# First mixer's projection with 512-column matmuls and folds on VectorE, and its first head's gate work one piece later

## The chip, the cores and the metric

One core of a Trainium2 chip runs the whole program. The metric is device time in microseconds (us), the median of several executions. The kernel before takes 2714.08 us (three executions, 2713.33 to 2714.75).

## The reference

Two decoder layers on 256 tokens with model width 2048, in float32. Layer 0 mixes tokens with a gated linear recurrence (8 heads of 256 channels), layer 1 with a state-space mixer; each is followed by a SwiGLU block and a gated per-layer embedding. What the change touches is the mixer of layer 0:

```python
xy = u @ w_in                                  # 2048 x 4096: this is phase A1
xr, yg = jnp.split(xy, 2, axis=-1)
yg = jax.nn.gelu(yg, approximate=True)
xr = causal_dwconv(xr, conv_w, conv_b)         # 4 taps
r = sigmoid(xb @ w_gate_r + b_gate_r)          # 256 x 256 for each head
i = sigmoid(xb @ w_gate_i + b_gate_i)
log_a = -8 * r * softplus(-lam); a = exp(log_a)
bterm = sqrt(-expm1(2 * log_a)) * (i * xr)
h[t] = a[t] * h[t-1] + bterm[t]                # scan over the tokens
y = h * yg                                     # then y @ w_out: phase A2
```

Here xb is xr by heads, and the `u` that enters is an RMS-normalised x.

## The kernel before

**Precision.** Each float32 operand is split in two parts, hi (rounded to the matmul's type) and lo (the rest), and a product is hi·hi + hi·lo + lo·hi. ScalarE makes the hi part of a weight piece (`hi`, L634), VectorE the lo part (`lo`, L915). TensorE does the three products of a 128x128 block in one of two forms. In the narrow form (`three`, L402 to L404) they are three matmuls of 256 columns into the same 256 columns of a bank. In the wide form (phases in the tuple `WIDE`, L419 and L421) one matmul of 512 columns multiplies the hi weights with the hi and lo tokens side by side into a bank's two halves, and one of 256 columns adds lo weights times hi tokens to the first half; whoever reads the bank must add the halves. `fold` (L1104) does this with one TENSOR_REDUCE on VectorE. The result is scaled by `rinv`, the norm of the token (a row is a tensor of 128 channels x 256 tokens).

**Order.** The program is a list of phases. A1 is the first: 4 iterations of 16 pieces, a piece being 8 blocks of weights (512 KB); an iteration holds two heads, and a head's 8 pieces make four groups of 16 blocks, two for xr (groups 0 and 1) and two for yg (2 and 3), each in its own bank. A2 follows with 32 pieces. Weights pass through a ring of 4 slots: SyncE's queue (SP) starts the load of a piece when the lo part four pieces back is made, ScalarE makes hi when TensorE has finished the piece four back, and VectorE lo. The loops of ScalarE and VectorE run over the same pieces as TensorE's, and at step q they split the piece q+3 (`LEAD`). Nothing plans the order: each engine executes its own written list, in order, and waits on semaphores.

**What a head needs beside its projection.** At the steps of its own 8 pieces (s = q % 8) VectorE reads group 0, 1, 2, 3 at s = 1, 3, 5, 7 (L1206 for xr into `xpad`, L1218 for yg into `yv`), does the convolution's later taps at s = 2 and 4 (`later_taps`, L1114 and L1116; the first tap is ScalarE's, L791), splits its input for the gates (`x_low`, L1005, at s = 4 and 6; `gates_low`, L1011, the gate weights, at s = 5). After the last piece of the head TensorE does the 24 gate matmuls, when both `x_low` of the head are done:

```python
pe.wait_ge(g_lo, head + 1)
pe.wait_ge(xc_lo, head * 2 + 2)
```

The rest is a chain one head later, `chain_step(head - 1, ...)`, shared between ScalarE and VectorE: ScalarE at s = 0 the gates' tanh (L702), at 1 the decays and a square (L711 to L721), at 3 the gelu's tanh (L729), at 5 a square root (L725), at 7 the hi part of y (L733); VectorE at s = 2 (L1124), 4 (L1129, L1133), 5 (L1137), and at 6 the input, the scan and y (L1141 to L1146). At the next s = 0 ScalarE starts with the hi part of a weight piece and then the next head's gates' tanh.

**First iteration.** Engines start with x and the norm still to come. The pieces of the first head come in another order (`HEAD_ORDER`), and its groups are read at q = 4 to 7. Its 24 gate matmuls stand after piece q = 9, its tanh is at q = 9 and its decays at q = 10, gelu at 11. On VectorE, `kk_steps(7)` (L933 to L1039, 13 small operations that make the decay's constants) stands at the end of q = 7, and `x_low` of the first head at q = 7 and 8.

Of the kernel before, what the change touches and what calls it, by code (L numbers as in the profile page):

```python
# [26 lines left out]
ALU = mybir.AluOpType  # L27
# [3 lines left out]
SEQ = 256  # L31
# [20 lines left out]
LAST_HEAD = {0: (0, 1), 1: (2, 3), 2: (4,), 3: (5,), 4: (6,), 5: (7,)}  # L52


WIDE = ("A2", "F1", "F2", "B2")
LAST = ((0, 4), (4, 4), (8, 4), (12, 2), (14, 2))
GELU_C = 0.7978845608028654
GELU_S = 0.044715 ** 0.5
# [65 lines left out]
def trunk(nc, t, out):  # L124
    with ExitStack() as ctx:
# [274 lines left out]
        def _(pe):  # L400
# [73 lines left out]
            for index, ph in enumerate(phases):  # L474
# [43 lines left out]
                def body(it, first, ph=ph, name=name, norm=norm, operand_ready=operand_ready):  # L518
# [5 lines left out]
                    for q, w in enumerate(ph["widths"]):  # L524
# [11 lines left out]
                        if name == "B1" and ph["half"] == 0 and first:  # L536
                            if q == 1:
                                decay_products()
                            if q == 9:
                                decay_columns()  # L540
                        if name == "A1" and q in ((9, 15) if first else (7, 15)):

                            head = it * 2 + q // 15 if first else it * 2 + q // 8
                            pe.wait_ge(g_lo, head + 1)
                            pe.wait_ge(xc_lo, head * 2 + 2)
                            if not (first and q == 9):
                                pe.wait_ge(gate_t, head * 4)
                            b = 0
                            for g in range(2):
                                for m in range(2):  # L550
                                    for k in range(2):
                                        tile, c = 16 + b // 2, slice((b % 2) * 128, (b % 2) * 128 + 128)
                                        mm = three(bank[4 + g][:, m * SEQ:(m + 1) * SEQ], R[1][:, 0, tile, c],
                                                   R[1][:, 1, tile, c], R[1][:, 0, 20 + k, :], R[1][:, 1, 20 + k, :],
                                                   k == 0, k == 1)
                                        b += 1
                            mm.then_inc(g_used, 1)
# [64 lines left out]
        def _(act):  # L622
# [38 lines left out]
            for index, ph in enumerate(phases):  # L661
# [73 lines left out]
                def chain_step(head, hh, s):  # L735

                    if s == 0:
                        gates(head)
                    elif s == 1:
                        decays(head)  # L740
                        gelu_square(head, hh)
                    elif s == 3:
                        gelu(head, hh)
                    elif s == 5:
                        mult(head)
                    elif s == 7:
                        lru_y(head, hh)

                def body(it, first, ph=ph, name=name, n=n, index=index):
                    last = isinstance(it, int) and it == ph["iters"] - 1  # L750
                    for q in range(n):
# [9 lines left out]
                            split_dt_weights(q // 13)  # L761
                        if name == "F2" and ph["half"] == 1 and last and q == 1:
                            split_p_high()
                        if name == "A1" and first and q == 9:
                            act.wait_ge(kk_done, 2)
                        if name in PAIRED and next_norm(ph) is not None and q > 8:
                            j = q - 9
# [17 lines left out]
                        if name == "A1":  # L785
                            head, hh, s = it * 2 + q // 8, q // 8, q % 8
                            taps_at = {5: 0, 6: 1} if first and q < 8 else {2: 0, 4: 1}
                            if s in taps_at:
                                j = taps_at[s]
                                act.wait_ge(bank_free, it * 8 + ph["group0"] + 4 + hh * 4 + j + 1)  # L790
                                nc.scalar.activation(xc[:, hh, j, :], xpad[:, j, 3:3 + SEQ], ACT.Identity,  # L791
                                                     bias=flat(apar[:, at(head * 2 + j), 4:5]),
                                                     scale=flat(apar[:, at(head * 2 + j), 3:4])).then_inc(atap_done, 1)
                            if not (first and q < 8):
                                chain_step(head - 1, 1 - hh, {0: 8, 1: 0, 2: 1}.get(s, s) if first else s)
                            if s in ((6, 7) if first and q < 8 else (3, 5)):
                                j = s - 6 if first and q < 8 else s // 5
                                act.wait_ge(xc_done, head * 2 + j + 1)
                                if not (first and q < 8):
                                    act.wait_ge(g_used, head)  # L800
                                nc.scalar.activation(R[1][:, 0, 20 + j, :], xc[:, hh, j, :], ACT.Copy).then_inc(xc_hi, 1)
                            if s == (2 if first and q < 8 else 4):
                                act.wait_ge(g_landed, head * 16 + 16)
                                if not (first and q < 8):
                                    act.wait_ge(g_used, head)
                                nc.scalar.activation(R[1][:, 0, 16:20, :],
                                                     graw[:, 0:1024].rearrange("p (k t) -> p k t", k=4), ACT.Copy
                                                     ).then_inc(g_hi, 1)
# [98 lines left out]
        def _(dve):  # L907
            own = Chain(dve, dve_own)
            V = nc.vector
# [119 lines left out]
            def kk_steps(q):  # L1029

                if q == 1:
                    softplus_mid(1, kt_b, kk_w, kk_z, kk_r)
                elif q == 7:
                    softplus_tail(kt_c, kk_w, kk_z, kk_r)
                    V.tensor_scalar(lam, kt_c, -4.0, None, ALU.mult).then_inc(kk_done, 1)
                    V.tensor_scalar(apar[:, :, 5:7], apar[:, :, 5:7], 0.5, None, ALU.mult).then_inc(kk_done, 1)

                    dve.wait_ge(params_in, 32)
                    own.link(V.tensor_scalar(bpar[:, :, 0:30], bpar[:, :, 0:30], 0.5, None, ALU.mult))  # L1039

            for index, ph in enumerate(phases):
# [60 lines left out]
                def fold(number, dst):  # L1102

                    own.link(V.tensor_reduce(dst, bank[number][:].rearrange("p (s t) -> p t s", s=2), mybir.AxisListType.X, ALU.add))  # L1104
# [44 lines left out]
                def body(it, first, ph=ph, name=name, n=n, index=index):  # L1149
                    last = isinstance(it, int) and it == ph["iters"] - 1  # L1150
                    for q in range(n):
# [31 lines left out]
                        if name == "A1":  # L1183
                            head, hh, s = it * 2 + q // 8, q // 8, q % 8
                            if s == 0 and not first:
                                y_low(head - 2, hh)
                            if first and q in (7, 8):
                                x_low(0, 0, q - 7)
                            if not (first and q < 8):
                                if s == 4:  # L1190
                                    x_low(head, hh, 0)
                                if s == 5:
                                    gates_low(head)
                                if s == 6:
                                    x_low(head, hh, 1)
                                chain_step(head - 1, 1 - hh, {2: 8, 3: 2}.get(s, s) if first else s)

                            group = ({4: 0, 5: 1, 6: 2, 7: 3} if first and q < 8 else {1: 0, 3: 1, 5: 2, 7: 3}).get(s)
                            if group is not None:
                                dve.wait_ge(w_used, HEAD_DONE[group] if first and q < 8 else p - s + 2 * group + 2)  # L1200
                                src = BANKS4[group]
                            if group in (0, 1):
                                j = group
                                tile = head * 2 + j
                                row = xpad[:, j, 3:3 + SEQ]
                                V.tensor_tensor(row, bank[src][:, 0:SEQ], rinv[:], ALU.mult).then_inc(bank_free, 1)  # L1206
                            taps_at = {5: 0, 6: 1} if first and q < 8 else {2: 0, 4: 1}
                            if s in taps_at:
                                j = taps_at[s]
                                tile = head * 2 + j  # L1210
                                dve.wait_ge(atap_done, tile + 1)
                                later_taps(xpad[:, j], xc[:, hh, j, :],
                                           lambda k, tile=tile: flat(apar[:, at(tile), k:k + 1]), xc_done)
                            if group in (2, 3):
                                if group == 2 and not first:
                                    dve.wait_ge(y_lo, head * 2 - 2)
                                row = yv[:, hh, group - 2, :]
                                V.tensor_tensor(row, bank[src][:, 0:SEQ], rinv[:], ALU.mult).then_inc(bank_free, 1)  # L1218
                            if first and q == 7:
                                kk_steps(q)  # L1220
                        if name in ("A2", "F2", "B2"):
                            per = n // 4
                            if q % per == per - 1 if name == "F2" else q >= 8:
# [146 lines left out]
                        V.scalar_tensor_tensor(out=zt[:, j, :], in0=zt[:, j, :], scalar=flat(bpar[:, at(group), 34 + j:35 + j]),  # L1370
                                               in1=grms[:], op0=ALU.mult, op1=ALU.mult).then_inc(yn_done, 1)

                steps(dve, ph, body, own, {"A1": 14, "B1": 22, "F1": 6, "PL": 0, "F2": 4}.get(name, 8))
                own.close()
            dve.wait_ge(h_done, 2 * KT)
            V.tensor_tensor(swi_u[:, 0, :], h[:, KT - 1, :], h[:, KT - 1, :], ALU.mult).then_inc(last_square, 1)
# [181 lines left out]
```

## Time and profile before

| what | value |
|---|---|
| median of three executions | 2714.08 us |
| the profiled execution | 2714.77 us |
| its span, first to last instruction | 2712.6 us |
| outside the span | 2.17 us |
| TensorE busy | 2680.7 us (99%) |
| VectorE busy | 1986.1 us (73%) |
| ScalarE busy | 1362.3 us (50%) |
| DMA, mean | 186 GB/s |
| granted TensorE clock, mean | 0.996 |

The page's busy times are averages over stages. Phase A1 lies in the first 235 us of the span, A2 behind it. Matmuls are pipelined: a record of a matmul is 0.28 us long, but they start 0.12 us apart, so distances between starts say how fast TensorE works, and records' lengths don't.

### The profile page before, as it was taken

The page shows a single profiled execution, that of the slowest core. Times are in us where ns is not written, and L with a number is a line of the kernel's source. Part 1 is how long each engine was busy: PE and PEld are TensorE (multiplying, and loading weights), DVE is VectorE, ACT ScalarE, POOL GpSimd, SP SyncE. Part 2 cuts the span into 40 slices and gives each one's busy share as a digit, 9 for nine tenths or more (in the row PEclk, how much of TensorE's full clock was granted, in tenths as well). Part 3 has the DMA queues.
Part 4 walks back from the last instruction along what each step waited for, and adds up shares of the span by engine and source line. Part 5 has one row for each costly group of instructions (what it writes and reads, how often), then busy time and mean ns, then how long its engine had stood idle before and what let it go on. Part 6 is the DMA issues. An engine that isn't in the chain of part 4 may idle for free.

```text
span 2712.6 us, 49802 instructions
## 1 busy us (share of the span) xinstructions
PE 2680.7 (99%) x17831; PEld 2454.5 (90%) x17831; DVE 1986.1 (73%) x2758; ACT 1362.3 (50%) x1832; POOL 306.9 (11%) x344
## 2 busy tenths in 40 slices
PE   8999999999999999999999999999999999999998
PEld 8999888888888889999998999988888888888897
DVE  6787776665666678888886788877666556666775
ACT  6776444444444444456664566644444444444453
POOL 1001300000000111200001000032000000001222
PEclk9999999999999999999999999999999999999999
DMA  5545565556665566555555655555555665555664
GB/s 198 186 163 194 177 196 188 190 175 188 206 190 188 191 188 194 186 173 190 183 187 180 205 179 183 186 179 187 190 190 181 182 206 189 188 190 175 189 196 136
DMA packets 154241, 504.70 MB, mean 186 GB/s; under 512 B 17104, under 2 KB 21520, under 8 KB 152976
## 3 DMA queue, kind: packets, MB, share of 16 engines
q1 hardware_dynamic: 154048, 503.14, 57.7%
q8 instruction: 70, 1.15, 0.2%
q14 instruction: 43, 0.35, 0.0%
q10 hardware_dynamic: 80, 0.07, 0.0%
HBM read 500.97 MB, written 2.16 MB: 185 GB/s over the span
## 4 chain that ended last, share of the span: by engine, by line
PE 95%; DVE 2%; ACT 1%; DMA 1%; issue 0%; SPq 0%; POOL 0%; DVEq 0%; POOLq 0%; ACTq 0%
PE bank L419 42%; PE bank L421 21%; PE bank L402 10%; PE bank L403 10%; PE bank L404 10%; DVE wlo L915 1%; ACT whi L634 0%; PE bank L597 0%; DMA wraw<-in_A 0%; DMA wraw<-in_B 0%; PE bank L588 0%; PE bank L599 0%; PE bank L575 0%; PE bank L580 0%; DVE arena L1114 0%
## 5 line engine op out<-in xcount | busy, mean ns | idle before, releaser
L419 PE MATMUL bank<-R,whi 128*128 128x512 f32 x4992 | 1734.1, 393 | 0.0
L915 DVE TENSOR_TENSOR wlo<-wraw,whi 128x1024 fp32r<-128x1024 f32 (+2 forms) x1008 | 1179.3, 1176 | 587.1 <-ACT whi L634 585.3
L634 ACT ACTIVATE whi<-wraw 128x1024 fp32r<-128x1024 f32 (+2 forms) x1008 | 985.6, 983 | 974.6 <-PE bank L421 738.3
L421 PE MATMUL bank<-R,wlo 128*128 128x256 f32 x4992 | 1390.4, 279 | 0.0
L419 PEld LDWEIGHTS bank<-R,whi 128*128 128x128 f32 x4992 | 935.1, 187 | 213.1 <-issue 0.3
L421 PEld LDWEIGHTS bank<-R,wlo 128*128 128x128 f32 x4992 | 940.2, 188 | 0.1
L402 PE MATMUL bank<-R,whi 128*128 128x256 f32 x2368 | 678.3, 286 | 6.8 <-DVE wlo L915 4.7
L403 PE MATMUL bank<-R,whi 128*128 128x256 f32 x2368 | 670.0, 283 | 0.0
L404 PE MATMUL bank<-R,wlo 128*128 128x256 f32 x2368 | 669.9, 283 | 0.0
L402 PEld LDWEIGHTS bank<-R,whi 128*128 128x128 f32 x2368 | 452.6, 191 | 13.3 <-DVE wlo L915 7.9
L403 PEld LDWEIGHTS bank<-R,whi 128*128 128x128 f32 x2368 | 452.7, 191 | 2.2 <-issue 1.9
L404 PEld LDWEIGHTS bank<-R,wlo 128*128 128x128 f32 x2368 | 452.6, 191 | 0.0
L1429 POOL TENSOR_TENSOR R<-arena,R 128x256 f32 x88 | 76.8, 873 | 1145.5 <-ACT R L819 1145.5
L1104 DVE TENSOR_REDUCE arena<-bank 128x256 f32<-128x512 f32 x176 | 121.5, 690 | 38.3 <-PE bank L421 36.0
L1410 POOL TENSOR_TENSOR square<-h 128x256 f32 x95 | 63.2, 665 | 638.6 <-DVE h L1230 488.3
L819 ACT ACTIVATE R<-arena 128x256 f32 (+1 forms) x88 | 36.8, 418 | 187.3 <-DVE arena L1257 187.3
L1411 POOL TENSOR_TENSOR sumsq<-sumsq,square 128x256 f32<-128x256 f32 x95 | 103.1, 1085 | 7.5
L1437 POOL TENSOR_TENSOR arena<-arena 128x512 f32<-128x512 f32 x8 | 10.9, 1363 | 463.5 <-ACT arena L888 463.5
L1114 DVE SCALAR_TENSOR_TENSOR arena<-arena,bpar 128x256 f32<-128x256 f32 x96 | 53.2, 554 | 9.3 <-ACT arena L846 4.9
L1229 DVE TENSOR_TENSOR h<-bank,h 128x256 f32<-128x256 f32 (+1 forms) x112 | 47.4, 423 | 9.5 <-PE bank L421 8.8
L956 DVE SCALAR_TENSOR_TENSOR R<-h,gains,R 128x256 fp32r<-128x256 f32 (+1 forms) x80 | 50.0, 624 | 3.7 <-DVE R L946 2.5
L1230 DVE TENSOR_TENSOR h<-bank,h 128x256 f32<-128x256 f32 (+1 forms) x112 | 47.5, 424 | 3.8
(175 smaller groups left out, 1252.9 us busy)
## 6 DMA issues: line engine op xcount, KB each, us to landing
wraw<-in_F SPq DMA_DIRECT2D x352, 512.0 KB, 3.5
wraw<-in_B SPq DMA_DIRECT2D x224, 512.0 KB, 3.3
wraw<-in_A SPq DMA_DIRECT2D x96, 512.0 KB, 3.8
wraw<-in_F SPq DMA_DIRECT2D x128, 384.0 KB, 3.1
wraw<-in_F SPq DMA_DIRECT2D x128, 320.0 KB, 3.2
wraw<-in_PL SPq DMA_DIRECT2D x64, 512.0 KB, 4.0
arena<-cs_rows SPq DMA_DIRECT2D x8, 1024.0 KB, 5.9
arena<-in_gates SPq DMA_DIRECT2D x8, 512.0 KB, 3.3
```

The source lines that it names most:

```text
L402: nc.tensor.matmul(dst, hi_w, hi_x, start=first, stop=False)
L403: nc.tensor.matmul(dst, hi_w, lo_x, start=False, stop=False)
L404: return nc.tensor.matmul(dst, lo_w, hi_x, start=False, stop=last)
L419: nc.tensor.matmul(dst.rearrange("p (s t) -> p s t", s=2), whi[:, q % RING, cols], src[:, :, k, :], start=first, stop=False)
L421: mm = nc.tensor.matmul(dst[:, 0:SEQ], wlo[:, q % RING, cols], src[:, 0, k, :], start=False, stop=last)
L634: nc.scalar.activation(whi[:, slot, 0:w * BLOCK], wraw[:, slot, 0:w * BLOCK], ACT.Copy).then_inc(w_hi, 1)
L915: V.tensor_tensor(wlo[:, slot, 0:w * BLOCK], wraw[:, slot, 0:w * BLOCK], whi[:, slot, 0:w * BLOCK].bitcast(F32), ALU.subtract).then_inc(w_ ...
L1104: own.link(V.tensor_reduce(dst, bank[number][:].rearrange("p (s t) -> p t s", s=2), mybir.AxisListType.X, ALU.add))
L1114: own.link(V.scalar_tensor_tensor(out=dst, in0=pad[:, k:k + SEQ], scalar=taps(k), in1=dst, op0=ALU.mult, op1=ALU.add))
L1410: own.link(G.tensor_tensor(square[:], flat(h[:, at(m), :]), flat(h[:, at(m), :]), ALU.mult))
L1411: G.tensor_tensor(sumsq[:], sumsq[:], square[:], ALU.add).then_inc(sumsq_done, 1)
L1429: G.tensor_tensor(flat(dst[:, 1, at(it * 2 + j), :]), swi_u[:, j, :], flat(dst[:, 0, at(it * 2 + j), :]).bitcast(F32), ALU.subtract).then_ ...
```

## The change

A1 joins the wide form. Its four reads of banks become a fold into the row and a multiplication by `rinv` in place. The number of VectorE's own semaphore steps of an iteration goes from 14 to 22 with the 8 folds. In the first iteration the gate matmuls stand after piece 10, ScalarE's steps of the first head are each one or two pieces later (tanh 10, decays 11, gelu 12), VectorE's L1124 is at 12 in place of 11, and `kk_steps(7)` comes at the end of q = 8, behind the second `x_low`.

```diff
-WIDE = ("A2", "F1", "F2", "B2")
+WIDE = ("A1", "A2", "F1", "F2", "B2")
 ... TensorE
-                        if name == "A1" and q in ((9, 15) if first else (7, 15)):
+                        if name == "A1" and q in ((10, 15) if first else (7, 15)):
-                            if not (first and q == 9):
+                            if not (first and q == 10):
                                 pe.wait_ge(gate_t, head * 4)
 ... ScalarE
-                        if name == "A1" and first and q == 9:
+                        if name == "A1" and first and q == 10:
                             act.wait_ge(kk_done, 2)
-                                chain_step(head - 1, 1 - hh, {0: 8, 1: 0, 2: 1}.get(s, s) if first else s)
+                                chain_step(head - 1, 1 - hh, {0: 8, 1: 8, 2: 0, 3: 1, 4: 3}.get(s, s) if first else s)
 ... VectorE
-                                chain_step(head - 1, 1 - hh, {2: 8, 3: 2}.get(s, s) if first else s)
+                                if first and s == 4:
+                                    chain_step(head - 1, 1 - hh, 2)
+                                chain_step(head - 1, 1 - hh, 8 if first and s == 2 else s)
                                 row = xpad[:, j, 3:3 + SEQ]
-                                V.tensor_tensor(row, bank[src][:, 0:SEQ], rinv[:], ALU.mult).then_inc(bank_free, 1)
+                                fold(src, row)
+                                V.tensor_tensor(row, row, rinv[:], ALU.mult).then_inc(bank_free, 1)
                                 row = yv[:, hh, group - 2, :]
-                                V.tensor_tensor(row, bank[src][:, 0:SEQ], rinv[:], ALU.mult).then_inc(bank_free, 1)
-                            if first and q == 7:
-                                kk_steps(q)
+                                fold(src, row)
+                                V.tensor_tensor(row, row, rinv[:], ALU.mult).then_inc(bank_free, 1)
+                            if first and q == 8:
+                                kk_steps(7)
-                steps(dve, ph, body, own, {"A1": 14, "B1": 22, "F1": 6, "PL": 0, "F2": 4}.get(name, 8))
+                steps(dve, ph, body, own, {"A1": 22, "B1": 22, "F1": 6, "PL": 0, "F2": 4}.get(name, 8))
```

## Rows read from the trace of the kernel before

**Rows 1.** Page, chain that ended last, by engine
```profile
PE 95%; DVE 2%; ACT 1%; DMA 1%; issue 0%; SPq 0%; POOL 0%; DVEq 0%; POOLq 0%; ACTq 0%
```

**Rows 2.** TensorE's waits, 0 to 240 us: releaser, total us, times, longest
```profile
PE bank L402 <- DVE R L1005: 4.8, 1, 4.8
PE bank L402 <- issue: 3.9, 1, 3.9
```

**Rows 3.** VectorE's timeline (start us, us, instruction, idle before): second x_low of heads
```profile
73.00 0.42 DVE L1005 TENSOR_TENSOR R<-arena,R 128x256 fp32r<-128x256 f32 x1
...
100.54 0.41 DVE L1005 TENSOR_TENSOR R<-arena,R 128x256 fp32r<-128x256 f32 x1
...
126.73 0.42 DVE L1005 TENSOR_TENSOR R<-arena,R 128x256 fp32r<-128x256 f32 x1
...
204.84 0.42 DVE L1005 TENSOR_TENSOR R<-arena,R 128x256 fp32r<-128x256 f32 x1
...
230.49 0.42 DVE L1005 TENSOR_TENSOR R<-arena,R 128x256 fp32r<-128x256 f32 x1
```

**Rows 4.** TensorE's timeline: first projection matmul of heads 2 and 3, first gate matmuls
```profile
78.78 0.30 PE L402 MATMUL bank<-R,whi 128*128 128x256 f32 x1
...
104.70 0.28 PE L402 MATMUL bank<-R,whi 128*128 128x256 f32 x1
...
127.74 0.28 PE L402 MATMUL bank<-R 128*128 128x256 f32 x1
...
231.59 0.28 PE L402 MATMUL bank<-R 128*128 128x256 f32 x1
```

**Rows 5.** ScalarE's timeline in a wide phase, one iteration of 64 blocks apart
```profile
382.97 0.42 ACT L819 ACTIVATE R<-arena 128x256 f32 x1 [0.71 <-DVE arena L1257]
...
405.16 0.42 ACT L819 ACTIVATE R<-arena 128x256 f32 x1 [0.71 <-DVE arena L1257]
```

**Rows 6.** VectorE's waits, 113.12 to 129.8 us
```profile
...
DVE arena L1114 <- DVE arena L1114: 0.3, 2, 0.2
```

**Rows 7.** VectorE's timeline in that stretch
```profile
113.11 1.23 DVE L915 TENSOR_TENSOR wlo<-wraw,whi 128x1024 fp32r<-128x1024 f32 x1 [2.02 <-ACT whi L634]
...
125.27 0.42 DVE L1218 TENSOR_TENSOR arena<-bank,rinv 128x256 f32<-128x256 f32 x1
125.60 1.22 DVE L915 TENSOR_TENSOR wlo<-wraw,whi 128x1024 fp32r<-128x1024 f32 x1
```

**Rows 8.** ScalarE's timeline behind it
```profile
129.92 0.64 ACT L733 ACTIVATE R<-arena 128x512 f32 x1 [3.80 <-DVE arena L1146]
...
131.52 1.28 ACT L702 ACT_TABLE_LOAD   x1
```

**Rows 9.** VectorE's timeline in a wide phase: a fold and what follows
```profile
386.69 0.69 DVE L1104 TENSOR_REDUCE arena<-bank 128x256 f32<-128x512 f32 x1 [0.45 <-PE bank L421]
387.41 0.42 DVE L1244 TENSOR_TENSOR arena<-arena,rinvh 128x256 f32<-128x256 f32 x1
387.78 1.23 DVE L915 TENSOR_TENSOR wlo<-wraw,whi 128x1024 fp32r<-128x1024 f32 x1
```

**Rows 10.** VectorE's timeline, first iteration
```profile
43.07 0.17 DVE L933 TENSOR_SCALAR arena<-arena 128x16 f32<-128x16 f32 x1
...
45.84 1.23 DVE L915 TENSOR_TENSOR wlo<-wraw,whi 128x1024 fp32r<-128x1024 f32 x1
```

**Rows 11.** ScalarE's timeline, first iteration
```profile
52.48 1.28 ACT L702 ACT_TABLE_LOAD   x1 [9.11 <-PE bank L404]
...
55.21 1.07 ACT L634 ACTIVATE whi<-wraw 128x1024 fp32r<-128x1024 f32 x1
...
59.66 1.06 ACT L634 ACTIVATE whi<-wraw 128x1024 fp32r<-128x1024 f32 x1
...
63.47 1.04 ACT L634 ACTIVATE whi<-wraw 128x1024 fp32r<-128x1024 f32 x1
```

**Rows 12.** TensorE in stretches of 0.25 us: busy (x), PEclk, DMA share, GB/s
```profile
72.00:72.25 0.25, 0.00 (x0) 0.50 0.70 147
```

## The prediction

> **What bounds the kernel now.** I read the page's chain first: 95% of it is TensorE [rows 1]. So a change in A1 counts by what it does to TensorE's starts, and next I read who made TensorE wait there. In A1 it stands still twice for long, 4.8 us and 3.9 us [rows 2]: once before the gate matmuls of head 0, once before those of head 1. "Issue" in the second row is the label of a wait that isn't resolved; the second `x_low` of head 1 starts at 73.00 [rows 3] and TensorE restarts when it is done, so both waits are for `x_low`. From head 2 on TensorE shows no wait before the gates, and VectorE is busy for only 73% of the span. It looks as if VectorE had room.
>
> The third view says that it hasn't. The second `x_low` of heads 2 and 3 start 26.19 us apart, the next three follow in 78.11 us (26.0 each), the last in 25.65 [rows 3]. TensorE's own need for a head is 127.74 - 104.70 = 23.04 us for 64 blocks and, at the same pace of 0.12 us a matmul, 2.88 us for the 24 of the gates, 25.92 us in all [rows 4]. So in the loop something other than TensorE sets VectorE's pace, and VectorE uses up a lead. It is a closed chain: ScalarE ends y's hi part (from 129.92), makes a weight piece, the gates' tanh (from 131.52) [rows 8], the next weight piece, the decays, and then the piece for which VectorE waits; that wait ended at 113.11 a head earlier, and from there VectorE works on to y [rows 7]. In that stretch it waits 0.3 us for results of its own and for no other engine [rows 6]. Two busy stretches, one behind the other, neither waiting for TensorE: their length is the head's period, whatever the averages say.
>
> **What the change does to TensorE.** A block takes 0.36 us now (23.04 / 64) and 22.19 / 64 = 0.347 us in a wide phase [rows 4, 5]: a head's projection gets 0.85 us shorter, its whole need falls to 25.07 us. The Trainium skill ("TensorE: Matmul & The Clock Gate", section "Wait — 56ns, not 53.3ns?") gives a matmul a fixed cost of about 2.5 ns beside its columns. One matmul less in each of 64 blocks would by that page bring 0.16 us a head (an estimate), and the last of my rivals would end at -2.9 us instead of -7.0. The rows disagree with it, and they decide.
>
> **What it adds to VectorE.** A fold and its multiplication take 387.78 - 386.69 = 1.09 us from start to start [rows 9]; the read that they replace takes 125.60 - 125.27 = 0.33 us [rows 7]. So +0.76 us for each of a head's four groups. By place, in the steady heads:
> - Group 0 (s = 1) is read when TensorE has done two pieces, and behind it VectorE waits 2.0 us for ScalarE [rows 7]: hidden. Without that wait it would cost 0.76.
> - Groups 1 and 2 (s = 3 and 5) lie in the stretch without waits, ahead of the second `x_low`. Twice 0.76, less some 0.06 for a piece of ScalarE's that comes just after the first: +1.46 us. Bounds: 0, if idle time that the rows don't show took them, and 1.8, if writing `xpad` and `yv` twice cost half a read more each than it does in rows 9. I take 1.46, from rows of the same two instructions.
> - Group 3 (s = 7) is read after y is handed to ScalarE, whose next two pieces come 1.6 and 5 us later; hidden except for a few tenths that the second of these covers.
>
> The period of a head is then 27.65 us in the loop and 27.1 us at the end, against TensorE's 25.07: about 2.6 us (2.0 at the end) of stall before each gate group. The 0.85 us saved lie inside that stall and are worth nothing. A later `gates_low` also holds SP's queue: the next gate load and the weight loads queued behind it wait for it. That costs nothing as long as it moves by one fold while y, after which ScalarE wants those pieces, moves by two. PSUM banks are no new wait: a group's bank is read a head's length before it is written again.
>
> **First iteration.** VectorE has no idle time to speak of from group 0's read on. The four folds put 3.04 us ahead of head 0's second `x_low`, and `kk_steps`, 45.84 - 43.07 = 2.77 us [rows 10], goes behind it, so that `x_low` stays near 47 us (0.2 us of a wait for ScalarE are filled). TensorE meanwhile does piece 10 (2.8 us), and its 4.8 us stall shrinks to three of 0.9, 0.9 and 0.2 us. At that place TensorE is 4.8 us ahead.
>
> But the next to be late is VectorE again, with head 1. Behind that `x_low` (47.4) it has `kk_steps` 2.77, a weight piece 1.14 and group 0's fold 1.09, and gives group 0 to ScalarE at 52.4. In ScalarE's list that group's first tap now stands ahead of the gates' tanh: tap 0.6 and tanh 2.73 (55.21 - 52.48) end at 55.8. Then come piece 14, the decays and a split, as before without the tap: 59.66 - 55.21 - 0.5 + 0.3 = 4.3 us, so piece 15's hi part starts at 60.1, where it started at 63.47 [rows 11]: 3.4 us early. VectorE follows it, but has two things more before head 1's second `x_low`: L1124, moved in from a piece earlier (0.6), and group 2's fold (0.76). So 73.00 becomes 73.00 - 3.4 + 1.4 = 71.0 or 71.1, and of the 4.8 us 1.9 are left. TensorE ends piece 15 at 65.2 and stands still for 6.4 us.
>
> **The clock.** In the 3.9 us stall before head 1's gates the granted clock went to 0.50 by 72.00 [rows 12], and from `x_low`'s end at 73.42 to head 2's first matmul at 78.78 [rows 3, 4] the 24 gate matmuls took 5.3 us in place of 2.88: the lower of the two levels, 1.2 GHz. After a longer stall they will again, so head 2 starts 1.9 us earlier too.
>
> **Sum.** Shift of the second `x_low`: head 1 -1.9; head 2 -1.9 + 1.46 = -0.4; then +1.46 at each of heads 3 to 7: +6.9 at head 7. Before, the last gates started 231.59 - 230.91 = 0.68 us after it ended [rows 3, 4]; now about 0.1: -0.6. A1's end, and all that follows it, is 6.3 us later. A2 has the wide form already and gives nothing back; VectorE's lead over TensorE there shrinks by those 0.6 us, which is what it could cost at most. In the profiled execution: 2712.6 + 6.3 + 2.2 outside the span = 2721.1. It was 0.7 us above the median, so the median becomes **2720.4 us**.
>
> Its own range: 1.46 may be 1.3 to 1.6 (-1.0 or +0.8 over six heads), the first iteration may be off by 1, the gates' low level may be left up to 0.9 earlier: 2718.3 to 2722.5. In 85 of 100 of it the result is over 0.2% slower; 0.2% (5.4 us) is about what a measurement of this kernel can tell from no change.
>
> **The rivals.**
> - **The clock falls in the new stalls too.** They are 2.0 to 2.6 us long; the one of 3.9 us had brought it to 0.50 after 2.3 us [rows 12], so they lie at the edge. Slow gates take up to 2.4 us more, and TensorE's next stall is then shorter, so it would be every other head (3, 5, 7). ScalarE has 131.52 - 127.15 = 4.4 us of its own work between `x_low` and the tanh [rows 3, 8] and would wait 1.2 us more; heads 3 and 5 cost 1.2 each, head 7 the full 2.4: +4.8, 2725.2. The Trainium skill (the same page, section "HAM oscillation — how this bites in real kernels") warns that stalls between groups of matmuls let TensorE fall back to half rate and pay for warming up again. 12%.
> - **One of the two folds is hidden** (+0.75 a head): -1.9 - 0.6 + 6 x 0.75 = +2.0, 2716.1. Against it: rows 6 show no idle time that would take it. 10%.
> - **Not slower: both are hidden.** The place is VectorE's stretch between its wait for ScalarE and the second `x_low`; the price is -1.9 - 0.6 = -2.5 us, 2711.6; it decides from a fold cost of 2.5 / 6 = 0.41 us a head downwards. The chain would need slack. 9%.
> - **The chain is no bound at all**, and heads follow TensorE's 25.07 us: -1.9 - 6 x 0.85 = -7.0, 2707.1. For it speaks that TensorE shows no wait from head 2 on; against it a period of 26.19 with a need of 25.92. 9%.
>
> **How the numbers follow.** Forecast 60%, rivals 12, 10, 9 and 9. Slower by over 0.2%: 0.85 x 60 + 12 = 63. Within 0.2%: 9 + 10 + 8 (of the third rival) = 27. Faster: 9 + 1 = 10. The range 2714.5 to 2725.5 takes in the forecast and the first two rivals and leaves out the last two.
>
> **What would show it.** Blocks 0.347 us apart in A1. VectorE's second `x_low` near 47 (head 0), 71 (head 1) and 100.1, then 27.6 us apart in the loop and 27.1 after it. TensorE waiting before the gates hardly at head 0, 6.4 us at head 1, 1.5 at head 2, 2.6 and 2.0 later. A2's first matmul 6.3 us later. I am wrong if the distances of `x_low` stay at 26.2 or fall to 25.1, or if VectorE is idle between s = 2 and s = 6 of a head.

## The result, and the profile after

The changed kernel takes 2720.1 us (median of 13 executions, 2719.22 to 2720.91) against 2714.55 us of the kernel before beside it: ratio 1.0022, 95% interval [1.0014, 1.0029]. It is slower by 5.5 us; 2720.4 had been forecast, in a range of 2714.5 to 2725.5. The profiled execution's span is 2718.4 us, 5.8 us more than before. Medians here and below are those of the fast executions; one of the kernel with group 1's fold doubled took 6802.85 us and is not counted.

TensorE's waits in the first 245 us of the changed kernel (columns: total us, times, longest), to be held against [rows 2] and, for the third line, against this one of the kernel before (0 to 240 us):

```profile
PE bank L402 <- DVE wlo L915: 3.3, 5, 1.0
```

```profile
PE bank L402 <- DVE R L1005: 9.2, 6, 1.9
PE bank L402 <- issue: 6.0, 1, 6.0
PE bank L419 <- DVE wlo L915: 6.0, 8, 1.4
```

The reader is to see six waits for `x_low` where there was one: the heads from 2 on, which had none. The 6.0 us are the stall before head 1's gates, and the 4.8 us before head 0's are gone. The waits for a lo part (`wlo`) all lie in the first iteration; they are 2.7 us longer in sum, mostly by the folds, for the new order without folds (below) has 3.8 us of them. The forecast had left 2.0 us of head 0's stall.

VectorE's timeline, the second `x_low` of heads 0 to 7, answering to [rows 3]:

```profile
46.69 0.42 DVE L1005 TENSOR_TENSOR R<-arena,R 128x256 fp32r<-128x256 f32 x1
...
70.75 0.42 DVE L1005 TENSOR_TENSOR R<-arena,R 128x256 fp32r<-128x256 f32 x1
...
98.85 0.42 DVE L1005 TENSOR_TENSOR R<-arena,R 128x256 fp32r<-128x256 f32 x1
...
126.45 0.42 DVE L1005 TENSOR_TENSOR R<-arena,R 128x256 fp32r<-128x256 f32 x1
...
154.05 0.42 DVE L1005 TENSOR_TENSOR R<-arena,R 128x256 fp32r<-128x256 f32 x1
...
181.65 0.42 DVE L1005 TENSOR_TENSOR R<-arena,R 128x256 fp32r<-128x256 f32 x1
...
208.78 0.42 DVE L1005 TENSOR_TENSOR R<-arena,R 128x256 fp32r<-128x256 f32 x1
...
235.83 0.42 DVE L1005 TENSOR_TENSOR R<-arena,R 128x256 fp32r<-128x256 f32 x1
```

Distances are 27.60 in the loop and 27.1 after it (28.10 from head 1 to head 2), where they were 26.19 and 25.65. Head 1 is 2.25 us early, head 7 is 5.3 us late. The links of the closed chain are seen around head 3, answering to [rows 8] on ScalarE and to [rows 7] on VectorE:

```profile
129.64 0.64 ACT L733 ACTIVATE R<-arena 128x512 f32 x1 [5.62 <-DVE arena L1146]
130.18 1.04 ACT L634 ACTIVATE whi<-wraw 128x1024 fp32r<-128x1024 f32 x1
131.24 1.28 ACT L702 ACT_TABLE_LOAD   x1
...
137.94 1.05 ACT L634 ACTIVATE whi<-wraw 128x1024 fp32r<-128x1024 f32 x1
```

```profile
136.23 0.68 DVE L1104 TENSOR_REDUCE arena<-bank 128x256 f32<-128x512 f32 x1
136.94 0.43 DVE L1209 TENSOR_TENSOR arena<-arena,rinv 128x256 f32<-128x256 f32 x1
139.02 1.23 DVE L915 TENSOR_TENSOR wlo<-wraw,whi 128x1024 fp32r<-128x1024 f32 x1 [1.65 <-ACT whi L634]
```

ScalarE goes from y (129.64) to the piece that VectorE waits for (137.94) without a pause. Group 0's fold at 136.23 stands ahead of a wait of 1.65 us: it costs nothing. A2's first matmul starts at 239.35, where it started at 234.47: A1 ends 4.9 us later. The other 0.9 us of the span come much later, in layer 1's mixer, where both kernels stall for 1.8 us (to 1195.18 before, to 1200.06 after). TensorE around and behind the stall (busy, count, granted clock, DMA share, GB/s), before and then after:

```profile
1190.00:1200.00 10.00, 8.23 (x69) 1.00 0.41 132
1200.00:1210.00 10.00, 10.00 (x85) 1.00 0.91 318
```

```profile
1200.00:1210.00 10.00, 9.94 (x70) 0.83 0.90 275
```

Behind the same stall the granted clock fell in one kernel and not in the other. It cost about 1.5 us (16 matmuls 0.21 us apart in place of 0.12), of which a short wait that only the kernel before has, at 1216, gives part back.

### The profile page after: what moved, and what is told of

Read it like the earlier page. It is cut to its first block, busy times and chain, and to the rows that moved or that the text cites. A ratio compares the mean times of both kernels' runs of the same rounds, so it can differ in the third digit from the quotient of the medians.

```text
span 2718.4 us, 48826 instructions
## 1 busy us (share of the span) xinstructions
PE 2677.3 (98%) x17319; PEld 2424.6 (89%) x17319; DVE 2007.4 (74%) x2790; ACT 1361.8 (50%) x1832; POOL 307.0 (11%) x344
## 4 chain that ended last, share of the span: by engine, by line
PE 90%; DVE 5%; ACT 2%; issue 1%; DMA 0%; SPq 0%; DVEq 0%; POOL 0%; ACTq 0%; POOLq 0%
PE bank L419 42%; PE bank L421 21%; PE bank L402 8%; PE bank L404 8%; PE bank L403 8%; DVE wlo L915 1%; ACT whi L634 1%; DVE arena L1114 1%; DVE arena L1104 0%; DMA wraw<-in_A 0%; PE bank L597 0%; DVE R L1011 0%; ACT L702 0%; ACT arena L702 0%; PE bank L588 0%
## 5 line engine op out<-in xcount | busy, mean ns | idle before, releaser
L419 PE MATMUL bank<-R,whi 128*128 128x512 f32 x5504 | 1916.9, 394 | 6.6 <-DVE wlo L915 6.0
L419 PEld LDWEIGHTS bank<-R,whi 128*128 128x128 f32 x5504 | 1031.3, 187 | 245.9 <-DVE wlo L915 9.3
L402 PE MATMUL bank<-R,whi 128*128 128x256 f32 x1856 | 533.0, 287 | 3.2 <-DVE arena L1304 1.8
L403 PE MATMUL bank<-R,whi 128*128 128x256 f32 x1856 | 525.9, 283 | 0.0
L402 PEld LDWEIGHTS bank<-R,whi 128*128 128x128 f32 x1856 | 355.1, 191 | 8.3 <-issue 4.3
L403 PEld LDWEIGHTS bank<-R,whi 128*128 128x128 f32 x1856 | 355.1, 191 | 2.1 <-issue 1.9
L1433 POOL TENSOR_TENSOR R<-arena,R 128x256 f32 x88 | 76.9, 874 | 1145.3 <-ACT R L819 1145.3
L1104 DVE TENSOR_REDUCE arena<-bank 128x256 f32<-128x512 f32 x208 | 143.4, 689 | 39.4 <-PE bank L421 37.1
```

The costliest lines, as they stand in the source:

```text
L402: nc.tensor.matmul(dst, hi_w, hi_x, start=first, stop=False)
L403: nc.tensor.matmul(dst, hi_w, lo_x, start=False, stop=False)
L419: nc.tensor.matmul(dst.rearrange("p (s t) -> p s t", s=2), whi[:, q % RING, cols], src[:, :, k, :], start=first, stop=False)
L1433: G.tensor_tensor(flat(dst[:, 1, at(it * 2 + j), :]), swi_u[:, j, :], flat(dst[:, 0, at(it * 2 + j), :]).bitcast(F32), ALU.subtract).then_ ...
```

## The experiments

Times are medians with the median of the kernel before from the same chip; the ratio is to that kernel. Every diff is against the changed kernel unless it says otherwise.

### The form alone, and the order alone

The kernel before with the wide form and the folds, and the kernel before with the first iteration's new order:

```diff
# form only, against the kernel before
-WIDE = ("A2", "F1", "F2", "B2")
+WIDE = ("A1", "A2", "F1", "F2", "B2")
-V.tensor_tensor(row, bank[src][:, 0:SEQ], rinv[:], ALU.mult)
+fold(src, row)
+V.tensor_tensor(row, row, rinv[:], ALU.mult)
# in both: DVE's number of semaphore steps to fit (22 with the folds, 14 without)
# order only: the same lines the other way round, against the changed kernel
```

> The 512-column form with its folds, but the first iteration's order left as it was before the change. My theory (VectorE and ScalarE form a closed chain, and groups 1 and 2's folds are in it): the second x_low of head 0 comes 3.0 us later than before (near 50.1 us), head 1's at 76.6 (73.00 + 2.8 + 0.8), steady distances 27.6 and 27.1 as in the changed kernel; A1 ends about 11 us later than before, so 2725 to 2727 us against 2714.5. Rival (the slowdown comes from the reordered first iteration, the form itself gains): not slower than before, about 2708 to 2714.

> The new order of the first iteration alone, with the narrow form and its plain reads. My theory: head 0's second x_low near 44.2 us, no stall of TensorE before head 0's gates, head 1's second x_low near 66.7 in place of 73.0, a stall of about 4 us before head 1's gates, and all later distances as before (26.2 and 25.7): 6 us faster than before, about 2708. Rival (the order of the first iteration is what costs): slower than before by 3 us or more, 2717 and up.

Form alone: 2725.39 against 2714.25, ratio 1.0042 [1.0028, 1.0055]: 11.1 us slower. `x_low` of heads 0 and 1 is at 49.8 and 76.9 (50.1 and 76.6 expected), from head 2 on 27.6 us apart. Order alone: 2707.79, ratio 0.9976 [0.9966, 0.9986]: 6.5 us faster, `x_low` at 44.5 and 67.1, distances of 26.2. So the change is two edits of opposite sign, -6.5 and +11.1. They add up to 4.6 us, against 5.5 measured together; the clock alone moves single executions by more than this difference (see the last section). The edit that puts the gate work later is the one that pays.

### Leaving out two folds, and moving one

```diff
+if group in (0, 3): fold(src, row); tensor_tensor(row, row, rinv)
+else: tensor_tensor(row, bank[src][:, 0:SEQ], rinv)           # no fold, groups 1 and 2
```
```diff
-group = {1: 0, 3: 1, 5: 2, 7: 3}.get(s)
+group = {1: 0, 3: 1, 6: 2, 7: 3}.get(s)                       # group 2 read late
```

> The changed kernel without the folds of groups 1 and 2 (their reads take only the first half of the bank, so one of the three products is left out for those rows; groups 0 and 3 still fold). My theory: the distance of the second x_low returns to 26.1 in the loop and 25.6 at the end, TensorE still stalls about 1 us before the gates although its own need is 25.07, and the time is 5 to 6 us below before, about 2709 (first iteration 2.3 us earlier, six heads 1.5 us each less than the changed kernel's 2720). Rival (the folds are harmless, something else in the 512-column form delays VectorE or ScalarE): distances stay at 27.6, time within 2.5 us of the changed kernel.

> The changed kernel with one move: the read of group 2 (fold and multiplication, 1.09 us) goes from s = 5 to behind the input, scan and y of s = 6, that is behind the second x_low and out of the closed chain, with the same work for VectorE. My theory: distances of x_low fall by 1.09 to 26.5 and 26.0, the whole by 7 x 1.1 = 7.6 us against the changed kernel: about 2712.5. Rival (VectorE's sum of work is what counts, not its place): no change against the changed kernel, 2720.

The first kernel leaves a product out: without the fold the rows of groups 1 and 2 lack hi weights times lo tokens, so it is no rival of the others. Its time is 2709.32, ratio 0.9982 [0.9973, 0.9991], with distances back at 26.2 and 25.6. With group 2 read late: 2712.72, ratio 0.9996 [0.9987, 1.0005], distances 26.5 and 26.0. The second kernel takes no work from VectorE; it only puts 1.09 us of it behind the `x_low` and y that others wait for, and the time falls by 7.4 us (7.6 expected).

### The same extra work at two places

```diff
+if group == 0 and not first:    # in the second kernel: group == 1
+    fold(src, row)
 fold(src, row)
```

> The changed kernel with group 0's fold done twice in every head from head 2 on: 6 x 0.72 = 4.3 us more work for VectorE, at the place that the prediction called hidden (behind it VectorE waits 1.65 us for ScalarE's weight piece). My theory: the distances of x_low stay at 27.6 and 27.1 and the time stays within 0.6 us of the changed kernel's 2720.1. Rival (VectorE's sum of work sets the pace): +4.3 us, 2724.4.

> The same extra work, 6 x 0.72 = 4.3 us, but group 1's fold is the one done twice, inside the stretch in which VectorE waits for nobody. My theory: distances of x_low grow by 0.72 to 28.3 and 27.8, the time by 4.3 us to 2724.4, perhaps 1 to 3 us more if the longer stalls (2.6 us by the trace) now lose the clock. Rival (sum of work): the same time as the kernel with group 0's fold doubled.

Group 0's fold twice: 2720.21 against 2714.15, ratio 1.002 [1.0011, 1.0029]: the changed kernel's time. In its profile `x_low` is 0.7 us late from head 2 on, which is the clock's doing: the gates of head 1 took 5.2 us in place of 4.5. From there the distances are the changed kernel's, 27.60 in the loop. Group 1's fold twice: 2725.52, ratio 1.004 [1.0027, 1.0053]: 5.3 us more for the same 4.3 us of work. In VectorE's timeline of the first of them the doubled fold eats the wait behind it, which falls from 1.65 to 0.93 us:

```profile
136.95 1.41 DVE L1104 TENSOR_REDUCE arena<-bank 128x256 f32<-128x512 f32 x2
138.39 0.43 DVE L1211 TENSOR_TENSOR arena<-arena,rinv 128x256 f32<-128x256 f32 x1
139.75 1.23 DVE L915 TENSOR_TENSOR wlo<-wraw,whi 128x1024 fp32r<-128x1024 f32 x1 [0.93 <-ACT whi L634]
```

In the second, TensorE's stalls are up to 2.6 us long. The clock falls behind two of them, those of heads 3 and 6 (2.6 and 2.1 us), about 1 us after TensorE has started again, and the distance to the next `x_low` is 0.5 to 0.6 us longer there: that is the part above 4.3. Behind head 5's stall, 2.6 us too, it does not fall. TensorE's waits from 100 to 240 us, and two stretches with their granted clock:

```profile
PE bank L402 <- DVE R L1005: 10.5, 5, 2.6
```

```profile
130.00:140.00 10.00, 10.00 (x56) 0.84 0.57 209
...
210.00:220.00 10.00, 7.89 (x44) 0.83 0.71 251
```

### Opening the chain

Three moves are made one on the other, all with group 2 read late. First y's hi part goes from s = 7 to s = 6 of the next head, so that ScalarE's path to the gates' tanh is free of it; then the gelu square behind the weight piece; then SP's gate load three pieces later. The last kernel has the first and the third, without the second. Of the first move the cut shows the main lines; A2's first pieces are changed to fit.

```diff
+act.wait_ge(y_done, head)                  # in gates(); tr, ti are still read by y
-lru_y(head - 1, ...) at s == 7;  y_low(head - 2) at s == 0
+lru_y(head - 2, hh) at s == 6;   y_low(head - 2) ahead of group 2's read
-decays(head); gelu_square(head, hh)        # s == 1
+decays(head)                               # s == 1; gelu_square behind hi() of s == 2
-if ph["name"] == "A1" and q % 8 == 2:      # SP, load of the gate weights
+if ph["name"] == "A1" and (q == 2 if first and q < 8 else q % 8 == 5):
```

> The kernel with group 2's read late, and in addition the closed chain is opened at one link: ScalarE no longer makes y's hi part and the next weight piece between y and the gates' tanh; y's hi part comes six pieces later (s = 6 of the next head, y's lo part right behind on VectorE), and the tanh waits for y and the gate matmuls alone. VectorE's and ScalarE's sums of work are unchanged. My theory: ScalarE starts the tanh 3.3 us after x_low's end in place of 4.37, so distances fall by 1.07 from 26.5 to 25.5 in the loop and to TensorE's own 25.1 to 25.3 at the end, 5.5 us less than the 2712.7 with group 2's read late alone: 2707, between 2706 and 2708.5. Rival (the path through y and ScalarE isn't the chain's link): no change, 2712.7.

> The kernel before this one in the list (group 2's read and y late), and ScalarE's gelu square (0.52 us) moved from ahead of the weight piece for which VectorE waits to behind it. My theory: the chain loses 0.5 us more and is now shorter than TensorE's need, so the distances are TensorE's 25.1 to 25.2 and TensorE stalls no more than 0.2 us before the gates: 1.5 us less, 2705.5. Rival (VectorE is now full, its work is 24.4 us a head beside its own waits): no better than the kernel without the square moved.

> The kernel with group 2's read, y and the gelu square late, and SP's load of the next head's gate weights moved three pieces later (q % 8 = 5 in place of 2; the first head's stays). In the two kernels before, ScalarE waited 4.5 us a head for a weight piece that lay behind that gate load in SP's queue, and the gate load waited for VectorE's gates_low. My theory: with the queue free, ScalarE has the piece in time, starts the tanh as soon as the gates are done, and the distances fall from 25.9 to TensorE's 25.1 to 25.2; A1 ends 3.8 us earlier than with the square late: 2705, between 2704 and 2706.5. Rival (VectorE is full, 24.4 us of work and 0.3 of its own waits in a head): distances stay above 25.6 and the time above 2707.

> Group 2's read and y late, as in the kernel that gained only 0.4 us, and the gate load moved three pieces later, but the gelu square in its old place. My theory: what kept y's move from paying was the weight piece that waited 4.5 us in SP's queue behind the gate load; with the load out of the way the chain is 26.53 - 1.07 = 25.5 us, just TensorE's own 25.5 in this phase (measured in the kernel with all moves), so distances of 25.5 to 25.6 and the time within 1 us of that kernel's 2708.2, 3.5 to 4 us below the same kernel with the early load (2712.3). Rival (the square's move is what paid, the load's didn't): 2711 or more.

| moves | median, us | ratio, interval |
|---|---|---|
| group 2 late | 2712.72 | 0.9996 [0.9987, 1.0005] |
| + y late | 2712.29 | 0.9990 [0.9981, 0.9999] |
| + y, square late | 2708.74 | 0.9977 [0.9968, 0.9986] |
| + y, square, gate load late | 2708.24 | 0.9976 [0.9967, 0.9986] |
| + y, gate load late | 2708.65 | 0.9981 [0.9972, 0.9990] |

Y late brought 0.4 us where I expected 5.5: a miss, and no more than noise, since its executions spread from 2709.51 to 2715.17. ScalarE's waits in that kernel, 100 to 182 us, show the wait that took the removed one's place:

```profile
ACT whi L634 <- DMA wraw<-in_A: 17.6, 4, 5.0
```

and SP's queue shows why. The gate load stands there until `gates_low` is done, and the weight pieces behind it with it:

```profile
123.49 0.33 SPq L363 DMA_DIRECT2D arena<-in_gates  x1
124.00 7.52 SPq L346 DMA_DIRECT2D wraw<-in_A  x4
```

ScalarE got its piece at 128.65, 4.5 us after it could have used it. As long as y came in between, this wait was covered. With the load moved, the wait for the piece is gone and ScalarE waits for TensorE (in the kernel with y and the gate load late, 100 to 182 us):

```profile
ACT L704 <- PE bank L404: 7.8, 4, 2.0
```

TensorE has no wait before the gates from head 2 on, and its gate groups start 25.6 us apart. The square's move alone brought 3.6 us while the load was early and 0.4 us with the load late; the load's move alone brought 3.6 us and, behind the square's, 0.5. So either of the two makes the chain about as short as TensorE's need, and the other then finds nothing left to take. Whether y has to be late at all once the load is moved was not tried.

The kernels with the square and the load late missed what I expected as well: 2708.74 for 2705.5, and 2708.24 for 2705 (2704 to 2706.5). The rival "VectorE is full" had been given times above 2707, but it was to show in distances above 25.6 too. With all moves the gate groups are 25.49 us apart, which is TensorE's own 64 x 0.353 + 24 x 0.12 us, and it waits for nobody from 80 to 228 us, while VectorE is busy for 95.46 of 101.95 us (98.34 to 200.29). VectorE is near its end there, but TensorE sets the pace; the miss is TensorE's pace, which comes next.

### The form where it pays

```diff
-if ph["name"] not in WIDE:
+if ph["name"] not in WIDE or ph["name"] == "A1" and isinstance(it, int):   # narrow in iteration 0
+if first: the plain read   else: fold and multiplication
```

> The kernel before this one in the list, but with the narrow form and plain reads in A1's first iteration (heads 0 and 1) and the 512-column form from head 2 on. In the first iteration TensorE waits for VectorE anyway and six folds stand on VectorE's path to head 1's second x_low. My theory: head 1's gates start near 67.4 in place of 70.6, everything after it 3.6 us earlier: 2701.5, between 2700.5 and 2703. Rival (the narrow form's slower TensorE costs as much as the folds there): no change.

> All the moves (first iteration's order, group 2, y, square and gate load late) with the narrow form and plain reads throughout A1. My theory: here TensorE sets the pace with 25.92 us a head, there are no stalls before the gates from head 2 on, and the moves bring nothing in the steady heads: within 1.5 us of the new first order alone (2707.8), 2706.7. So the 512-column form from head 2 on is worth 6 x 0.85 = 5.1 us once VectorE's chain is short. Rival (the moves are what pays, the form is worth nothing): as fast as the kernel with a narrow first iteration.

Narrow in the first iteration, wide after it, with all moves: 2704.24 us (5 executions, 2703.71 to 2705.82) against 2714.21, ratio 0.9964 [0.9950, 0.9977]. It beats both kernels, by 10 and by 16 us. I had expected 2701.5, from 2700.5 to 2703: a miss, and inherited, for against the kernel with all moves it gained 4.0 us where 3.6 were expected. Narrow throughout with all moves: 2707.38, ratio 0.9975 [0.9966, 0.9984]. The form in the steady heads is worth about 3 us once VectorE's chain is short, not the 5.1 I had counted. The reason is TensorE's pace. In the kernel with all moves, where nothing stalls it, its timeline has

```profile
160.32 0.40 PE L419 MATMUL bank<-R,whi 128*128 128x512 f32 x1
...
161.02 0.40 PE L419 MATMUL bank<-R,whi 128*128 128x512 f32 x1
...
161.73 0.40 PE L419 MATMUL bank<-R,whi 128*128 128x512 f32 x1
...
162.44 0.40 PE L419 MATMUL bank<-R,whi 128*128 128x512 f32 x1
```

These rows are two blocks apart each: 0.353 us a block, and not the 0.347 of [rows 5]. By that pace six heads gain 6 x 0.43 = 2.6 us.

## Why the prediction was right

**The closed chain: right, and shown.** That the second `x_low` sets the pace, that groups 1 and 2 are on the chain and groups 0 and 3 are not, was tested by taking work away (folds left out), by moving work with nothing taken away (group 2 late), and by adding the same work at groups 0 and 1 (0 against 5.3 us). That group 3 is off the chain was not tested by itself.

**Cost of the folds: right in size.** 27.60 - 26.19 = 1.41 us a head in the loop, 27.05 - 25.65 = 1.40 at the end; I had 1.46.

**First iteration: right in place and nearly in size.** `x_low` at 46.7 and 70.75 were forecast near 47 and at 71.0 to 71.1, TensorE's stall at 6.4 us, and it was 6.0. The two edits alone confirm that the order gains and the folds eat it.

**The term that was mis-sized** is the clock's: I let the gates after the stall run at the lower level as long as before, so head 2 would start 1.9 us early. It started at 75.72, 3.1 us early; the low level ended 3.4 us after the restart, not 5.3 [rows 3, 4]. In both kernels it lasted 6.8 us in all, from 72.0 to 78.8 before and from 67.9 to 74.7 now. It began 2.3 us into the stall of the one and 2.6 us into that of the other, so the longer stall took up more of it. I had put 0.9 us of this into the forecast's own range. A1 ended 4.9 us late and not 6.3: some 0.9 us of the difference are the clock's, 0.35 come from head 1's earlier `x_low` and 0.3 from folds of 1.41 in place of 1.46. The 0.9 us that the clock took back in layer 1 was in no term. That the total came out as near as it did, 5.8 against 6.3 in the span, is luck to that extent.

**The forecast's own range** doesn't follow from its terms: as they are listed they give 2717.5 to 2722.2, not 2718.3 to 2722.5. The result lies in both.

**TensorE's need: wrong, without effect.** I took the wide form's pace from the feed-forward phase, 0.347 us a block. In A1 it is 0.353, so a head gains 0.43 us and not 0.85, and the stalls in the loop were 1.9 us and not 2.6. A2, next door and wide already, has the same 0.353: its matmuls would have told. The fixed 2.5 ns for a matmul that the Trainium skill gives ("TensorE: Matmul & The Clock Gate", section "Wait — 56ns, not 53.3ns?") is under both measurements. It would give 0.16 us a head (an estimate); A1's rows give 0.43 and rows 5 give 0.85.

**The rival of the clock** did not happen: behind none of the three stalls of 1.9 us did it fall. In the kernel with group 1's fold doubled it fell behind two of three stalls of 2.1 to 2.6 us. That the shorter stalls are why it spared the changed kernel is likely but not shown, since a stall of 1.8 us in layer 1 lost it.

## What to carry to other kernels

Where the bounding engine shows no wait, look at the distances of a recurring instruction that it depends on: here they were 26.19 us with a need of 25.92, so another chain already set the pace and was using up a lead, and an average of 73% hid it. Before you add work to an engine that is "free for a quarter of the time", find the stretch between its last wait and the instruction that others wait for. Here work inside it cost its full length in every head (1.41 us for two folds), work outside it cost nothing as long as it fitted into a wait, and moving 1.09 us of it out shortened the head by 1.07. When a link of such a chain is taken out, read the queue of loads as well: here a load that waited on a semaphore held a weight piece back for 4.5 us a head.

## What the runs showed of the hardware that I had not expected

- At a granted clock of 1.00 a wide pair on one block runs at one of two paces, 0.353 or 0.347 us. In the kernel before it is 0.353 through all of A2 and changes to 0.347 when the feed-forward phase begins (near 330 us); two later stretches of wide matmuls, behind narrow phases, begin at 0.353 and change after some 10 us (near 1440 and 1780 us). In the two kernels that have all moves and the wide form, head 2 runs at 0.347 and the heads behind it at 0.353. The narrow form's three matmuls took 0.360 in all phases. What sets the pace wasn't tried and stays open.
- The same 1.8 us stall in layer 1 was followed by a fallen clock (0.83 over the next 10 us) in the changed kernel and not in the kernel before; stalls of 1.9 us in A1 never brought it down, stalls of 2.1 to 2.6 us did in two of three. At head 1's stall the lower level lasted 6.8 us from fall to rise in twelve of the fourteen kernels and 3.4 us in two, and the gates behind it took 4.2 to 5.3 us. So they differ by up to 1.1 us, and layer 1 by up to 1.5 us (from 0.65 less to 0.84 more than in the kernel before). Only for a part of this is there an edit that explains it. Smaller differences between kernels can't be read from the total of one profile.
